# A table of slots built by one-hot products on TensorE, a third buffer of normalised rows and four ring places in the scan

## The reference

```python
def step(s, inp):                       # one chunk of 64 positions of the scan
    u_c, w_c, qk_c, qd_c, kd_c, dl_c = inp
    v_new = u_c - einsum(w_c, s)
    o_c = einsum(qd_c, s) + einsum(qk_c, v_new)
    s = s * dl_c + einsum(kd_c, v_new)
    return s, o_c

def _hier_moe(h, w_rc, w_rf, w_eu, w_ed):       # h = rmsnorm(x), 1056 tokens
    g_sel = argmax(softmax(tok @ w_rc))           # 1 of 4 groups
    top_w, top_i = top_k(softmax(fine[g_sel]), 2) # 2 of its 8 experts
    ...
    act = silu(gate) * up * combine_w
    out = out + einsum('nef,efd->nd', act, w_ed)
x = x + _hier_moe(_rmsnorm(x, norm_ffn_w), ...)
```

## Time and profile before

| what | us |
|---|---|
| median of 3 runs | 1480.87 (1478.59 to 1483.13) |
| profiled execution, its own time | 1484.7 |
| span of the profiled execution | 1483.0 |
| PE busy | 1376.6 (93%) |
| DVE busy | 731.8 (49%) |
| ACT busy | 389.9 (26%) |
| POOL busy | 164.1 (11%) |

### The profile page before, as it was taken

One profiled execution on the slowest core, in us unless ns is written; L12 is line 12 of the kernel. 1 busy time (PEld: TensorE's weight loads), 2 busy tenths in 40 slices (PEclk: granted clock), 3 DMA queues, 4 the chain that ended last, 5 costly groups with the idle time before them and its releaser, 6 DMA issues.

```text
span 1483.0 us, 28178 instructions
## 1 busy us (share of the span) xinstructions
PE 1376.6 (93%) x12076; PEld 958.6 (65%) x12076; DVE 731.8 (49%) x1371; ACT 389.9 (26%) x707; POOL 164.1 (11%) x174
## 2 busy tenths in 40 slices
PE   7999999999999999999977899998986999999976
PEld 6667667666666566655677766674445788888862
DVE  4676693502434523588688544345543432333326
ACT  4211200113627552232112310010111233333323
POOL 1000000000001000044226200002223011111110
PEclk9998999999999999999989999999997999999997
DMA  5244486622111112052551425153343999999949
GB/s 165 77 111 66 124 237 184 153 72 73 47 31 31 45 32 90 29 138 57 165 175 39 128 84 192 46 190 121 114 156 135 408 420 414 419 410 424 415 178 351
DMA packets 172289, 250.16 MB, mean 169 GB/s; under 512 B 62574, under 2 KB 142836, under 8 KB 163708
## 3 DMA queue, kind: packets, MB, share of 16 engines
q1 hardware_dynamic: 148736, 200.67, 40.4%
q0 software_dynamic: 9888, 29.90, 5.3%
q10 hardware_dynamic: 13532, 17.70, 3.4%
HBM read 185.70 MB, written 66.47 MB: 170 GB/s over the span
## 4 chain that ended last, share of the span: by engine, by line
PE 80%; DVE 10%; ACT 3%; issue 3%; DMA 3%; POOL 2%; ACTq 0%; SPq 0%; POOLq 0%; DVEq 0%
PE P L760 28%; PE P L1336 7%; PE P L1234 6%; PE P L1305 4%; PE P L1074 4%; PE P L1144 4%; PE P L1333 4%; PE P L925 2%; PE P L1270 1%; PE P L1309 1%; POOL arena L645 1%; PE P L1191 1%; DVE arena L1642 1%; PE P L987 1%; PE P L956 1%
## 5 line engine op out<-in xcount | busy, mean ns | idle before, releaser
L760 PE MATMUL P<-arena 128*128 128x352 f32 x1680 | 522.5, 466 | 4.0 <-ACT arena L2417 2.8
L760 PEld LDWEIGHTS P<-arena 128*128 128x128 f32 x1680 | 316.9, 192 | 185.1 <-issue 24.8
L1336 PE MATMUL P<-arena 128*32 128x128 f32 x1536 | 175.0, 274 | 0.0
L1333 PE MATMUL P<-arena 128*32 128x384 f32 x1536 | 172.9, 490 | 0.1
L1336 PEld LDWEIGHTS P<-arena 128*32 128x32 f32 x1536 | 165.9, 110 | 0.3
L1305 PE MATMUL P<-arena 128*32 128x512 f32 (+1 forms) x768 | 89.5, 488 | 1.5 <-DVE arena L2063 1.5
L1234 PE MATMUL P<-arena 128*128 128x512 f32 x192 | 90.5, 618 | 0.0
L1309 PE MATMUL P<-arena 128*32 128x256 f32 x384 | 88.7, 380 | 0.0
L2006 DVE COPY arena<-P 128x512 f32<-128x512 f32 x24 | 16.6, 692 | 108.0 <-PE P L1270 106.3
L2554 ACT ACTIVATE arena<-P 32x128 f32<-32x128 f32 x96 | 26.0, 271 | 143.8 <-PE P L1336 143.1
L1333 PEld LDWEIGHTS P<-arena 128*32 128x32 f32 x1536 | 60.7, 110 | 3.9 <-issue 0.4
(11 more groups left out here) (423 smaller groups left out, 1900.6 us busy)
## 6 DMA issues: line engine op xcount, KB each, us to landing
arena<-in_w_expert_up_dram SPq DMA_DIRECT2D x32, 2048.0 KB
arena<-in_w_expert_down_dram SPq DMA_DIRECT2D x32, 1024.0 KB, 8.2
arena<-in_w_in_dram SPq DMA_DIRECT2D x36, 512.0 KB
x_d<-zero SPq DMA_DIRECT2D x4, 3072.0 KB, 22.5
arena<-x_d POOLq DMA_DIRECT2D x24, 512.0 KB
gate_d<-arena ACTq DMA_DIRECT2D x16, 528.0 KB, 4.7
arena<-gate_d SPq DMA_DIRECT2D x24, 352.0 KB, 3.1
arena<-in_x_prompt_dram SPq DMA_DIRECT2D x16, 512.0 KB, 5.5
```

What stands on the lines that cost most here:

```text
L760: m = pe.matmul(P[:, b + j, 0:TBK], w[:, k, :], hT[:, k, TBK * j:TBK * j + TBK], start=f, stop=l)
L1333: m = pe.matmul(P[strip_of(s), i % 2, 0:384], rows_of[s], WU[i % NWE][:, k, 128:512], start=k == 0, stop=k == KD - 1, skip_group_check=True)
L1336: m = pe.matmul(P[RT:128, i % 2, 128 * s:128 * s + 128], rows_of[s], WU[i % NWE][:, k, 0:128], start=k == 0 and s == 0, stop=k == KD - 1, ...
```

## The change

The token numbers of the first 3072 slots no longer go through DRAM. For each tile and each of a token's two choices, DVE splits the slot number into `quot` (which group of 128 slots, 24 of them) and `rest` (which slot in the group), and makes two one-hot tiles: `in_chunk` (128 x 2 x 128) from `rest`, and `chunk_of` (128 x 2 x 24) from `quot`, the latter times the token number plus one. PE multiplies one by the other (`slots_found`), in the spare columns of the bank of the next tile's `places`, and DVE adds the result to `slot_table`. The last tile's product takes the place of the transpose behind expert 1, with four DVE instructions in place of the cast. POOL's eighteen scatters to idx_d, SP's wait for them and the read-back go; idx_d is still cleared, and still used when an expert overflows 96 rows, which does not happen with these inputs.

`h2` has three buffers (`NH2 = 3`). The waits for the scatters and stores of an older tile move from DVE to ACT, which now writes the squares into the h2 buffer instead of `junk`, and ask for tile p - 3. The scan's rings have four places of 256 columns instead of two, 512 columns apart, and POOL waits for chunk c - 4.

```diff
-        KB = [at(i * 512, HP, C) for i in range(2)]
+        NRING = 4
+        KB = [at(i * HP * C, HP, C) for i in range(NRING)]
...
-                    if c >= 2:
-                        pool.wait_ge(used, c - 1)
+                    if c >= NRING:
+                        pool.wait_ge(used, c - NRING + 1)
...
-                if p < TT_ - 1:
-                    slots_taken(p)
...
-                    if c == 1:
-                        slots_taken(TT_ - 1)
...
+            def slots_found(o, i):
+                n = rows(WORD[i])
+                pe.wait_ge(s_pos, 2 * i + 2)
+                for j in range(2):
+                    m = pe.matmul(o, in_chunk[i // (TT_ - 1)][0:n, j, :], chunk_of[0:n, j, :], start=j == 0, stop=j == 1)
+                return m
+
             def places(i):
                 pe.wait_ge(s_M, i + 1)
                 bank = bank6()
+                if i > 0:
+                    slots_found(bank[:, 2 * E:2 * E + NFIRST], i - 1)
                 m = pe.matmul(bank[:, 0:E], later[:], Mt[:, WORD[i], :], start=True, stop=i == 0)
...
-                        pe.wait_ge(s_idn, 16)
-                        pe.transpose(bank6()[:, 0:NFIRST], idx_n[0:NFIRST], ident[0:NFIRST, 0:NFIRST]).then_inc(s_6, 1)
+                        slots_found(bank6()[:, 0:NFIRST], TT_ - 1).then_inc(s_6, 1)
...
-                    read6(ins)
+                    link(ins)
+                    if p > 0:
+                        link(dve.tensor_tensor(slot_table, slot_table, bk[:, 2 * E:2 * E + NFIRST], ALU.add))
+                    dve.sem_inc(s_6f, 1)
...
-                dve.wait_ge(s_pos, p + 1)
+                dve.wait_ge(s_pos, 2 * p + 1)
+                link(dve.tensor_scalar(quot, pos[:, :, i], 1 / 128, -63.5 / 128, ALU.mult, ALU.add))
+                link(dve.tensor_scalar(quot, quot, MAGIC, MAGIC, ALU.add, ALU.subtract))
+                link(dve.scalar_tensor_tensor(rest, quot, -128.0, pos[:, :, i], ALU.mult, ALU.add))
+                link(dve.tensor_tensor(in_chunk[p // (TT_ - 1)], columns.unsqueeze(1).broadcast_to([128, 2, 128]),
+                                       rest.unsqueeze(2).broadcast_to([128, 2, 128]), ALU.is_equal))
+                link(dve.tensor_tensor(chunk_of, tilef[:, 0:NFIRST].unsqueeze(1).broadcast_to([128, 2, NFIRST]),
+                                       quot.unsqueeze(2).broadcast_to([128, 2, NFIRST]), ALU.is_equal))
+                dve.tensor_tensor(chunk_of, chunk_of, tokf1[:, :, i].unsqueeze(2).broadcast_to([128, 2, NFIRST]),
+                                  ALU.mult).then_inc(s_pos, 1)
+                dve.wait_ge(s_pos, 2 * p + 2)
...
-                if p >= 2:
-                    dve.wait_ge(s_h2d[p % 2], 32 * (p // 2))
-                    dve.wait_ge(s_h2s[p % 2], H2S[p % 2] + 16 * (p // 2))
-                    dve.wait_ge(s_7, N7_R(p - 2))
...
-                if p >= 2:
-                    act.wait_ge(s_h2, p - 1)
-                act.activation(junk[0:n, :], x1[0:n, i, :], ACT.Square, accum_out=st[0:n, a:a + 1]).then_inc(s_sq3, 1)
+                if p >= NH2:
+                    act.wait_ge(s_h2d[p % NH2], 32 * (p // NH2))
+                    act.wait_ge(s_h2s[p % NH2], H2S[p % NH2] + 16 * (p // NH2))
+                act.activation(h2[p % NH2][0:n, :], x1[0:n, i, :], ACT.Square, accum_out=st[0:n, a:a + 1]).then_inc(s_sq3, 1)
...
-                if lo == 0:
-                    sp.wait_ge(s_sct, 16 * 2 * TT_)
-                    sp.dma_start(idx_n[0:NFIRST], idx_d[0:E * RT].rearrange("(t p) a -> t (p a)", p=128)).then_inc(s_idn, 16)
```

More of the change, by code:

```diff
@@ L202, in hybrid_step @@
         gS, bS, dS, oS = at(r + 4736, TS), at(r + 4740, TS), at(r + 4744, 32), at(r + 4776, TS, 32)
-        KB = [at(i * 512, HP, C) for i in range(2)]
-        KDr = [at(1024 + i * 512, HP, C) for i in range(2)]
-        VB = [at(2048 + i * 512, HP, C) for i in range(2)]
+        NRING = 4
+        KB = [at(i * HP * C, HP, C) for i in range(NRING)]
+        KDr = [at(1024 + i * HP * C, HP, C) for i in range(NRING)]
+        VB = [at(2048 + i * HP * C, HP, C) for i in range(NRING)]
         wT = [at(3072 + i * 512, HP, C) for i in range(2)]
@@ L287, in hybrid_step @@
         xr = [at(q + 2336 + i * D, D) for i in range(2)]
-        h2 = [at(q + 4384 + i * D, D) for i in range(2)]
+        NH2 = 3
+        h2 = [at(q + 4384 + i * D, D) for i in range(NH2)]
         yout = [at(q + 4384 + i * D, D) for i in range(4)]
@@ L318, in hybrid_step @@
         tot, tiles, incl, before, cnt, e_slot = [small(E) for _ in range(6)]
+        PX = sb("PX", [128, 4, 2, C])
+        columns, in_first, in_second = [PX[:, i].rearrange("p a b -> p (a b)") for i in range(3)]
         zero = sb("zero", [128, 128])
@@ L328, in hybrid_step @@
         tokg_i = small(NCHUNK).bitcast(I32)
-        tokf, desf, tilef, idx_n, o_te = small(2, TT_), small(EG), small(NTILE), small(128)[0:NCHUNK], small(NOV)
+        tokf, tokf1, desf, tilef, idx_n, o_te = small(2, TT_), small(2, TT_), small(EG), small(NTILE), small(128)[0:NCHUNK], small(NOV)
+        quot, rest = small(2), small(2)
+        chunk_of, slot_table = small(2, NFIRST), small(NFIRST)
+        in_chunk = [PX[:, 1:3].rearrange("p i a b -> p i (a b)"), h2T[1][:, 0:2, :]]
         assert off[0] <= ARENA, off[0]
-        PX = sb("PX", [128, 4, 2, C])
-        columns, in_first, in_second = [PX[:, i].rearrange("p a b -> p (a b)") for i in range(3)]
         N1 = sb("N1", [128, 4, HP, NC_])
@@ L437, in hybrid_step @@
         s_h2 = sem("s_h2")
-        s_h2d = [sem("s_h2d0"), sem("s_h2d1")]
-        s_h2s = [s_ygd, s_U]
-        H2S = [16 * L * 4, 16 * L]
+        s_h2d = [sem(f"s_h2d{b}") for b in range(NH2)]
+        s_h2s = [s_ygd, s_U, sem("s_h2s2")]
+        tiles_in = lambda b, count: (count + NH2 - 1 - b) // NH2
+        H2S = [16 * L * 4, 16 * L, 0]
         s_io = sem("s_io")
@@ L654, in _ @@
             pool.wait_ge(s_yz, 1 + 16 * X_PARTS)
-            def slots_taken(p):
-                i = WORD[p]
-                n = rows(i)
-                if p == 0:
-                    pool.wait_ge(s_zid, 16)
-                for j in range(2):
-                    pool.indirect_dma_start(idx_d, bass.IndirectOffsetOnAxis(pos_i[0:n, j, i:i + 1], 0), tokf[0:n, j, i:i + 1],
-                                            None, bounds_check=E * RT - 1, oob_is_err=False).then_inc(s_sct, 16)
             for p, i in enumerate(WORD):
@@ L671, in _ @@
                 for j in range(2):
[L672 to L673 removed]
+                    pool.indirect_dma_start(x_d, bass.IndirectOffsetOnAxis(pos_i[0:n, j, i:i + 1], 0), h2[p % NH2][0:n, :],
+                                            None, bounds_check=E * RT - 1, oob_is_err=False).then_inc(s_h2d[p % NH2], 16)
                 if p == TT_ - 2:
[L675 to L676 removed]
+                    for b in range(NH2):
+                        pool.wait_ge(s_h2d[b], 32 * tiles_in(b, TT_ - 1))
                     pool.dma_start(xg_first, x_d[0:128, :]).then_inc(s_xg[0], 16)
[L678 to L682 removed]
+            for b in range(NH2):
+                pool.wait_ge(s_h2d[b], 32 * tiles_in(b, TT_))
             def further_rows():
                 pool.wait_ge(s_idx, 1)
[L686 to L687 removed]
+                pool.wait_ge(s_zid, 16)
+                for b in range(NH2):
+                    pool.wait_ge(s_h2s[b], H2S[b] + 16 * tiles_in(b, TT_))
                 for i in range(TT_):
@@ L1057, in w_chunk @@
                     for h in heads:
-                        i = pe.matmul(bank[h, 64 * hp:64 * hp + 64], KB[c % 2][h, hp, :], TB[hp][h, c, :], start=True,
+                        i = pe.matmul(bank[h, 64 * hp:64 * hp + 64], KB[c % NRING][h, hp, :], TB[hp][h, c, :], start=True,
                                       stop=True)
@@ L1068, in u_chunk @@
                     for h in heads:
[L1069 removed]
+                        pe.matmul(P[h, c % 2, 64 * hp:64 * hp + 64], TB[hp][h, c, :], VB[c % NRING][h, hp, :],
                                   start=hp == 0, stop=False, skip_group_check=True)
@@ L1108, in _ @@
                     for h in heads:
-                        i = pe.matmul(bank[h, 64 * hp:64 * hp + 64], KDr[c % 2][h, hp, :], vn[c % 2][h, hp, :],
+                        i = pe.matmul(bank[h, 64 * hp:64 * hp + 64], KDr[c % NRING][h, hp, :], vn[c % 2][h, hp, :],
                                       start=True, stop=True)
```

38 lines of the change are left out of this document (17 added, 21 removed).

## The result

The changed kernel takes **1470.63 us** (median of five runs, 1467.83 to 1472.16), the kernel before 1482.02 us beside it (median of five, 1478.59 to 1485.79). The ratio is 0.9919, 95% interval 0.9905 to 0.9932. The forecast was 1485.2 with a range from 1477 to 1490: wrong in sign and outside the range. The profiled execution's span is 1469.4 us, against 1483.0.

A forecast was written before the change was run, and what follows sets the result against it. PE bounds the experts, PE and DVE in turn the handover, W_O and scan. W_O and handover +4.8, scan -0.9 + 0.4, sum +4.3 us: 1489.0 for the profiled execution, 1485.2 for the median; range 1477 to 1490.

The forecast's parts named there:

- W_O, fifth to eighth tile: W_O: DVE's new work fits in its slack; PE's table matmuls cost 4 x 0.36 = 1.5 us, upper bound 3.1.
- The forecast's own sign of being wrong: Forecast wrong if TensorE's clock in W_O lay clearly off 0.95, or the scan's length fell by over 3 us.
- The price of the table: Per tile: DVE 1.6 us for six instructions, 0.22 for the addition; PE 0.36 at full clock, 0.9 at half.
- fourth tile: W_O: DVE is late; six new instructions and the addition make PE's transposes start 1.8 us later.
- Handover: Between W_O and the experts: +1.6 normalisation, +0.9 table at half clock, +0.2 chunk 1, -1.6 chunk 2, +0.2 behind expert 1.
- -1.6 for chunk 2: Handover: chunk 2 is requested at once, ahead of the weights, so PE's 1.59 us wait goes; -1.6 us.
- chunk 1's term: Handover: the addition delays the slots, the scatter and chunk 1, for which PE already waits 1.16 us; +0.2 us.
- second rival: W_O and handover: longer waits bring TensorE to half clock in two further stretches; 1489 us, chance 0.2.
- the head norms of chunk 12 run alone, -0.9: Scan's end: POOL's last five instructions come earlier, so these head norms take 2.2 us against 3.1; -0.9 us.
- One collision at the start, +0.4: Scan's start: six extra POOL instructions run beside the sample recurrence, which is on the path; +0.4 us.
- first rival: Scan: POOL really holds it, so deeper rings remove all 8.3 us of PE's idle time; 1477.4 us, chance 0.15.
- Third buffer: Normalised rows: removes DVE's waits for scatters and stores of tile p - 2, which cost no idle time; 0 us.

The follow-up runs named there:

- the kernel with the numbers put off: Kernel before, with the token-number scatters of tiles 0 to 6 delayed until the square of the tile after next has run; 1464.0 us.
- the kernel with the wait without effect: Kernel before, with a wait for the next tile's square ahead of the token-number scatters; that square had already run, so issue times stayed the same; 1481.9 us.
- the numbers first: Changed kernel with POOL's two token-number scatters per tile put back, ahead of the scatters of rows; 1486.4 us.
- the numbers put back: Changed kernel with POOL's two token-number scatters per tile (tiles 0 to 7) put back behind the scatters of rows; 1483.3 us.

## Why the prediction was wrong, step by step

**The step that failed** is "W_O, fifth to eighth tile" and with it the whole treatment of POOL in W_O. The forecast saw the pauses in the router, with the row at 1012.09, and took them for something of PE's own: a possible price for the table's matmuls, never a possible gain. It asked of the removed scatters only what was queued behind them (chunk 2, SP's wait). Laying POOL's timeline beside PE's in that stretch would have shown it: each of the five long pauses in the routers (1.13 to 1.15 us) begins while an indirect transfer is being issued. It cost 13.5 us of routers and 5.1 of clock. The forecast's own sign of being wrong, a clock in W_O clearly off 0.95, came only faintly: the granted clock was 0.95 before and is 0.98.

**The price of the table was right.** Six instructions on DVE: 1101.82 to 1103.37 in the last tile, 1.55 us against 1.6. The addition takes 0.18 and its slot 0.33 with what follows, against 0.22. On PE 0.36 at full clock (1035.46 to 1035.82) and 0.87 at half clock (1114.34 to 1115.21), against 0.36 and 0.9. The sum for W_O can be tested against the kernel with the numbers put off, which has no table and pauses of only 1.0 us: 127.57 - 122.44 = **5.1 us**, forecast 5.1 (5.5, if the 0.4 us by which the changed kernel's routers are shorter are allowed for). By parts: from the first matmul to the third tile's transposes (the forecast's "fourth tile") +1.9 (forecast 1.8), from there to the eighth tile's +1.7 (1.5), the last +1.5 (1.8 with the ninth tile's 0.2). In the first of these the wait of about 2 us that the forecast looked for shows as two, 0.56 us ahead of the table's matmuls and 0.68 ahead of the transposes. The table is the change's only cost in W_O, and it could have been saved there: putting the scatters off gives the same freedom from pauses without it, though its handover is 2.8 us longer than that of the kernel before (322.27 us against 319.49 from the last transposes to the last scatter), where the changed kernel's is 1.9 longer.

**Handover.** PE's timeline of the changed kernel:

```profile
1105.59 1.97 PE L1152 MATMUL P<-shift_id,arena 128*128 128x128 f32 x8 [6.10 <-DVE arena L1926]
1114.34 1.05 PE L1170 MATMUL P<-arena,PX 128*128 128x24 f32 x4 [4.91 <-DVE arena L1869]
...
1130.02 1.09 PE L1271 MATMUL P<-shift_id,arena 128*128 128x128 f32 x8 [1.87 <-DMA arena<-x_d]
...
1145.24 1.02 PE L1170 MATMUL P<-arena 128*128 128x24 f32 x4 [1.89 <-DVEq L2077]
1146.19 0.86 PE L1334 MATMUL P<-arena 128*32 128x384 f32 x3
```

Against the earlier trace rows: the normalisation's wait grew from 4.83 to 6.10, the half-clock table is there, chunk 1 is waited for 1.87 instead of 1.16 us (forecast +0.2, measured +0.7), chunk 2's wait of 1.59 is gone, the one behind expert 1 stays (1.98, now 1.89). From the last transposes on -0.3 was forecast and +1.9 measured. At first sight most of the difference is the last row: the matmuls behind the table's last product run at half clock. These 4 us (columns as above) have a granted clock of 0.61, so that 3.1 of them ran at half and about 1.6 us were lost:

```profile
1145.59:1149.59 4.00, 4.00 (x45) 3.60 (x48) 0.72 (x4) 0.00 (x0) 0.00 (x0) 0.61 1.06 442
```

The kernel before has 1.00 in the same place. But neither this stretch nor the missing wait for chunk 2 needs the change. The kernel before with four ring places has the old queue of POOL, two scatters between chunk 1 and chunk 2, and no table:

```profile
1135.19 1.00 POOL L663 DMA_INDIRECT idx_d<-arena  x1 [0.30 <-issue]
1136.50 0.99 POOL L663 DMA_INDIRECT idx_d<-arena  x1 [0.30 <-issue]
1137.47 0.60 POOL L715 DMA_DIRECT2D arena<-x_d  x1
```

```profile
1147.29 1.09 PE L1271 MATMUL P<-shift_id,arena 128*128 128x128 f32 x8
```

```profile
1153.62:1157.62 4.00, 4.00 (x46) 3.61 (x50) 0.18 (x1) 0.00 (x0) 0.00 (x0) 0.58 0.97 411
```

PE doesn't wait for chunk 2 there either, and the half-clock stretch follows behind expert 1 all the same; the kernel with the wait without effect shows both too. From the last transposes to the last scatter these two take 319.61 and 319.58 us, and the kernel before, with the wait and without the stretch, 319.49. So the forecast's -1.6 for chunk 2 was not there to be gained in sum: the wait is in two of the five traces with the old queue and in none of the nine with the new one, and in 11 of the 12 traces without it the stretch comes in its place. That the wait is gone "as forecast" was partly luck. Against the two kernels that share the stretch the changed one is 1.8 us behind: the table at half clock is 0.9, chunk 1 is 0.7, and the rest comes at the product behind expert 1. The forecast had 0.9, 0.2 and 0.2 for these, so what it had wrong in the handover is the gain of 1.6 and the size of chunk 1's term.

With two ring places, the same code as the changed kernel from there on, chunk 1 is waited for 1.16 us, neither this stretch nor the one behind chunk 1 (which the kernel before has too) came, and the stretch took 318.13 us; why the clock stayed up in that one trace is open. The second rival, that longer waits bring TensorE to half clock in further stretches, is therefore not shown: the further stretch is there in kernels without the longer waits too.

**Scan.** The step "the head norms of chunk 12 run alone, -0.9" was right: the last head norms take 0.59 us as forecast and PE's wait fell from 1.70 to 0.80. "One collision at the start, +0.4" did not come in this trace (in two of the ten with four places the first chunk is 0.4 us longer), and the half-clock stretch, which the forecast had only in its bound of -3, did go: -2.6 instead of -0.5 in these two traces. The first rival, that POOL really holds the scan, is refuted: the 8.3 us in nine places are 7.8 us in nine in the changed kernel.

**Third buffer** worth 0: right. The Trainium skill's rule on the shared interfaces of GpSimd and VectorE (GPSIMD Engine Reference, section "1. Specifications") would, with the price that the forecast took from rows 9, have let the new comparison lose up to 0.4 us; it took 0.42 to 0.43 us in all nine tiles, also where it ran beside POOL's issue, no loss.

With the pauses and their clock priced at 13.5 and 5.1, and the scan's stretch at 1.6, the same sum would have given +4.3 - 18.6 - 1.6 = -15.9 us, against -13.6 in the spans; the 2.2 us missing in the handover are most of what is left.

## To carry over

Pauses of TensorE that no semaphore explains are not a constant of the program: lay the other engines' timelines beside them before taking them as given. Where TensorE runs many narrow matmuls in a row, keep indirect transfers of POOL's queue from being issued during it; moving them beside wide matmuls costs one wait and here gave 5.1 us more in that phase than making them unnecessary by other means. A wait that is absent after a change counts as its gain only if it stays in the kernels without the change. Whoever removes an operation should price not only what waits behind it but what runs beside it.

## What the runs showed of the hardware

- While POOL issues an indirect transfer (0.98 us for 128 rows), and up to 0.8 us beyond, TensorE's narrow matmuls come about five in 0.73 us, with pauses of 0.45 us, instead of 64 in 0.70 us. The first 41 to 46 of a router run at full speed all the same. Rows in flight from such a transfer, plain transfers from POOL's queue and POOL's arithmetic have no such effect.
- Wide matmuls (128x512) beside the same transfers keep their time: eight in 3.60 us while such transfers were issued.
- Behind some of the slow routers the granted clock falls to half for a part of the next wide matmuls, 1.7 us lost each time: behind three of six in the kernel before, two with the numbers first, one with the numbers put back, none where the routers stay short. Which ones is not explained here.
- Up to the scan's first chunk, in code that none of the kernels changes, profiled executions take 761 to 767 us. So single medians of a few runs don't rank kernels here that differ by 2 us.
